# Eight forget-gate columns: from a split weight job to whole 32-bit products in four groups of output rows

## What is computed

```python
h = _rmsnorm_2(x, g_mix)                       # x: 512 x 1024, the first block's output
proj = h @ w_in                                # 1024 -> 5128 columns, split into
qa, ka, va, qb, kb, vb, fl, ga, gb = jnp.split(proj, IN_OFFSETS, axis=-1)
log_f = jax.nn.log_sigmoid(fl + b_forget)      # fl: only 8 columns, one for each head
cum = jnp.cumsum(log_f, axis=1)                # goes into the scores of the second attention
```

## Time and profile before

| | |
|---|---|
| three runs | 1702.13, 1702.26, 1707.29 us; median 1702.26 |
| span of the profiled execution | 1703.5 us |
| TensorE busy | 1661.9 us (98% of the span), 10010 matmul instructions |
| VectorE, ScalarE, GpSimd busy | 940.9, 764.6, 631.7 us |
| mean granted clock of TensorE | 0.997 |
| moved by DMA | 181.68 MB |

### The profile page before, as it was taken

The page is one execution under the profiler, slowest core; times in us unless marked ns, Lnnn a source line. Parts: engine busy times, 40 slices in busy tenths (PEclk is TensorE's granted clock), DMA queues, the critical chain, the costliest instruction groups (busy, mean ns, idle before and its releaser), DMA issues. The chain is left out here.

```text
span 1703.5 us, 26528 instructions
## 1 busy us (share of the span) xinstructions
PE 1661.9 (98%) x10010; PEld 1408.0 (83%) x10010; DVE 940.9 (55%) x1657; ACT 764.6 (45%) x1326; POOL 631.7 (37%) x439
## 2 busy tenths in 40 slices
PE   6999999999999999999999999999999999999998
PEld 4987777778888889978987788798787788989896
DVE  5326566544445258847546664777545565555552
ACT  5324554532223234566545655444445324535351
POOL 1027767342220086643113332965100227323242
PEclk9999999999999999999999999999999999999998
DMA  7322122133333223345632110224411222222221
GB/s 323 112 88 68 55 74 80 63 129 123 106 116 123 99 83 102 105 179 189 233 119 80 50 50 30 96 100 177 169 50 52 98 99 99 100 99 98 99 100 50
DMA packets 29802, 181.68 MB, mean 107 GB/s; under 512 B 3352, under 2 KB 5784, under 8 KB 10112
## 3 DMA queue, kind: packets, MB, share of 16 engines
q1 hardware_dynamic: 22136, 150.12, 24.5%
q10 hardware_dynamic: 7560, 30.09, 5.1%
HBM read 169.57 MB, written 10.50 MB: 106 GB/s over the span
## 5 line engine op out<-in xcount | busy, mean ns | idle before, releaser
L438 PE MATMUL acc<-rarena,wh 128*128 128x512 f32 (+1 forms) x1720 | 657.7, 382 | 6.9 <-DVE rarena L1792 1.3
L440 PE MATMUL acc<-rarena,wl 128*128 128x512 f32 (+1 forms) x1720 | 642.3, 373 | 0.0
L439 PE MATMUL acc<-rarena,wh 128*128 128x512 f32 (+1 forms) x1720 | 641.9, 373 | 0.0
L438 PEld LDWEIGHTS acc<-rarena,wh 128*128 128x128 f32 x1720 | 323.9, 188 | 87.7 <-issue 23.5
L440 PEld LDWEIGHTS acc<-rarena,wl 128*128 128x128 f32 x1720 | 323.8, 188 | 62.1
L439 PEld LDWEIGHTS acc<-rarena,wh 128*128 128x128 f32 x1720 | 324.2, 188 | 56.4 <-issue 0.5
L320 DVE TENSOR_TENSOR wl<-raw,wh 128x2048 fp32r<-128x2048 f32 x81 | 197.2, 2434 | 239.7 <-ACT wh L314 239.6
L314 ACT ACTIVATE wh<-raw 128x2048 fp32r<-128x2048 f32 x99 | 188.9, 1908 | 76.0 <-PE acc L440 69.4
L2555 POOL TENSOR_TENSOR wl<-raw,wh 128x512 fp32r<-128x512 f32 x78 | 105.0, 1375 | 91.2 <-ACT wh L1330 91.2
L320 POOL TENSOR_TENSOR wl<-raw,wh 128x2048 fp32r<-128x2048 f32 x18 | 82.6, 4591 | 149.4 <-ACT wh L314 149.4
L516 PE MATMUL acc<-wh,rarena 128*128 128x256 f32 x336 | 94.2, 280 | 2.7 <-DVE rarena L1792 2.5
(11 more groups left out here) (346 smaller groups left out, 3083.2 us busy)
## 6 DMA issues: line engine op xcount, KB each, us to landing
raw<-in_w SPq DMA_DIRECT2D x129, 1024.0 KB, 4.8
early<-in_wmod SPq DMA_DIRECT2D x8, 1024.0 KB, 19.8
farena<-in_gate ACTq DMA_DIRECT2D x4, 1024.0 KB, 4.8
mkv_scratch<-rarena ACTq DMA_DIRECT2D x2, 2048.0 KB, 12.0
rarena<-mkv_scratch ACTq DMA_DIRECT2D x1, 4096.0 KB, 15.0
farena<-in_rpb ACTq DMA_DIRECT2D x16, 240.0 KB, 3.8
farena<-in_x_grid SPq DMA_DIRECT2D x2, 1024.0 KB, 6.9
o_scratch<-early ACTq DMA_DIRECT2D x8, 256.0 KB, 2.0
```

The costliest lines, as they stand in the source:

```text
L438: mm(o, w[0], m[0], start=start, stop=False)
L439: mm(o, w[0], m[1], start=False, stop=False)
L440: return mm(o, w[1], m[0], start=False, stop=stop)
```

## The change

The job `FL` is taken out of the table, so that 128 jobs are left, and with it its three-part products and its split. The 8 columns come as a small array `fl` (128 x 8 x 8) by a transfer of their own, are scaled once by the norm's gains on VectorE (`fl_w`), and are multiplied as plain 32-bit numbers with the residual rows `y`, tile k into output rows 32 (k mod 4) to 32 (k mod 4) + 7 of bank `T[0]`. So four partial results, each of two tiles, stand in four groups of output rows; ScalarE copies them out (four instructions into `fl_t`), and VectorE adds them up (three additions) before it multiplies by `rstd`. The products stand ahead of the column sums; the spread moves behind the first V2 group; that group now waits for `h2_ready` tile by tile.

```diff
--- before.py
+++ after.py
@@ -23,7 +23,7 @@
 
 
 PHASES = [("V", 4, 24), ("QK", 8, 24), ("CONV", 16, 32), ("ZB", 4, 8), ("GO", 16, 32),
-          ("WO", 4, 8), ("MKV", 8, 16), ("FL", 1, 1), ("V2", 4, 16), ("DQK", 4, 8), ("FQK", 4, 8),
+          ("WO", 4, 8), ("MKV", 8, 16), ("V2", 4, 16), ("DQK", 4, 8), ("FQK", 4, 8),
           ("GO2", 12, 32), ("WO2", 4, 8), ("QM", 4, 8), ("OM", 4, 8), ("MLP", 32, 64)]
 JB, GB = {}, {}
 _j = _g = 0
@@ -189,6 +189,7 @@
         xin = view(early, 16, (KT, SEQ))
         rstd, tmp = F(24, SEQ), F(26, SEQ)
         fl_t = [F(16 + 2 * n, SEQ) for n in range(4)]
+        fl_w = F(29, KT, 8)
         ptile2, strip2, odiff = [F(0, SEQ), F(2, SEQ)], [F(4, SEQ), F(6, SEQ)], F(8, 16, 128)
         osb2 = [F(16, 128), F(16.5, 128)]
         subsq, gsub, zmask = F(17.5, 128), F(18, 128), F(19, SEQ)
@@ -882,21 +883,15 @@
                 if c == 0:
                     pe.wait_ge(s_("accy_done"), KT)
                     column_sums(S[1], acc_sq, 4, True, True).then_inc(s_("sum_done"), 1)
-                if c == 7:
-
-                    pe.wait_ge(s_("acc1_done"), KT)
-                    column_sums(S[1], acc_sq, 4, True, True).then_inc(s_("sum_done"), 1)
-
-
-            base, g = JB["FL"], GB["FL"]
-            pe.wait_ge(s_("lo_done"), base + 1)
-            acc_wait_free(pe, 0, 2, g)
+
+
+            pe.wait_ge(s_("h2_ready"), 5)
             for k in range(KT):
-                pe.wait_ge(s_("h2_ready"), k + 1)
-                last = mm3(acc[g % 2][:], wt(base % 2, k, 0), at(h2, slice(None), k), k == 0, k == KT - 1)
-            last.then_inc(s_("acc_ready"), 1)
-            pe.wait_ge(s_("ncol_ready"), 4)
-            spread(S[0], rcol, 4)
+                pe.wait_ge(s_("sq1_ready"), 2 * k + 2)
+                r = 32 * (k % 4)
+                mm(T[0][r:r + 8, :], fl_w[:, k], y[:, k], start=k < 4, stop=k >= 4)
+            pe.wait_ge(s_("acc1_done"), KT)
+            column_sums(S[1], acc_sq, 4, True, True).then_inc(s_("sum_done"), 1)
 
 
             for c in range(4):
@@ -904,7 +899,11 @@
                 pe.wait_ge(s_("lo_done"), base + 1)
                 for b in range(4):
                     token_group(base, g + b, 0, 2,
-                                lambda k, b=b: at(h2, slice(None), k, slice(128 * b, 128 * b + 128)))
+                                lambda k, b=b: at(h2, slice(None), k, slice(128 * b, 128 * b + 128)),
+                                "h2_ready" if c == b == 0 else None)
+                    if c == b == 0:
+                        pe.wait_ge(s_("ncol_ready"), 4)
+                        spread(S[0], rcol, 4)
 
 
             def project(job, u):
@@ -1391,6 +1390,7 @@
 
             act.wait_ge(s_("merged_ready"), KT)
             act.dma_start(mem, A["mem"]).then_inc(s_("mem_in"), 16)
+            act.dma_start(fl_w, A["fl"]).then_inc(s_("mem_in"), 16)
             act.wait_ge(s_("gtp_ready"), 1)
             for m in range(KT):
                 if m % 2 == 0 and m > 0:
@@ -1399,7 +1399,7 @@
                     half = slice(4 * m - 8, 4 * m - 4)
                     act.dma_start(xin[:, half], A["x_natural"][:, half]).then_inc(s_(f"xin{m - 2}"), 16)
                 if m == 1:
-                    act.wait_ge(s_("mem_in"), 16)
+                    act.wait_ge(s_("mem_in"), 32)
                     f(sqm, mem, ACT.Square).then_inc(s_("sqm_ready"), 1)
                 if m == 4:
                     act.wait_ge(s_("summ_done"), 1)
@@ -1451,13 +1451,12 @@
             act.dma_start(mkv_dram[:, 16 * 256:], mkv_all[:, 16 * 256:]).then_inc(s_("rows_spilled"), 16)
 
 
-            split_hi(act, 0, 2, JB["FL"] + 1)
             z, az, lf = fl_t[0][0:8], fl_t[1][0:8], fl_t[3][0:8]
 
 
-            act.wait_ge(s_("ncol_ready"), 4)
-            acc_wait_ready(act, 0, 2, GB["FL"])
             act.wait_ge(s_("spread_done"), 4)
+            for r in range(4):
+                f(fl_t[r][0:8], T[0][32 * r:32 * r + 8, :], ACT.Copy)
             f(rstd, S[0][:], ACT.Copy).then_inc(s_("rstd_ready"), 1)
             for c in range(4):
                 split_hi_half(act, JB["V2"] + c + 1, 0)
@@ -2106,6 +2105,8 @@
             for c in range(4):
                 split_job(v, 0, 2, JB["WO"] + c + 1)
                 if c == 2:
+                    v.wait_ge(s_("mem_in"), 32)
+                    tt(fl_w, fl_w, vec(P_MIX, 8).rearrange("p (k n) -> p k n", n=1).broadcast_to([128, KT, 8]), MUL)
                     v.wait_ge(s_("rmsm_ready"), 1)
                     link(nc.vector.reciprocal(rstd_m, rstd_m))
                     for k in range(KT):
@@ -2149,15 +2150,14 @@
                     x1_tile(KT + 1)
 
 
-            split_job(v, 0, 2, JB["FL"] + 1)
             invert(rcol, 4)
             v.wait_ge(s_("ncol_ready"), 4)
             z, m0, cum = fl_t[0][0:8], fl_t[2][0:8], fl_t[3][0:8]
-            g = GB["FL"]
-            acc_wait_ready(v, 0, 2, g)
             v.wait_ge(s_("rstd_ready"), 1)
-            free_acc(tt(z, acc[g % 2][0:8], rstd[0:8], MUL), g)
-            wait_evacuated(v, 0, 2, g)
+            tt(z, z, fl_t[1][0:8], ADD)
+            link(tt(m0, m0, cum, ADD))
+            link(tt(z, z, m0, ADD))
+            link(tt(z, z, rstd[0:8], MUL))
             link(ts(z, z, par[0:8, P_BF:P_BF + 1], None, ADD))
             ts(m0, z, 0.0, None, MIN).then_inc(s_("fl_ready"), 1)
 
@@ -2726,9 +2726,6 @@
     ga, gb = _pair_cols(win, seq(64, 4)), _pair_cols(win, seq(72, 4))
     jobs += oc + oa + [w for pair in zip(ga, gb) for w in pair]
     jobs += square(i["w_o"][0]) + square(i["w_kv_mem_2"][0], 8)
-    fl = np.zeros((KT, 128, JW), np.float32)
-    fl[:, :, 0:8] = win2[:, 3072:3080].reshape(KT, 128, 8)
-    jobs += [fl.transpose(1, 0, 2)]
     jobs += _pair_cols(win2[:, :3072], seq(8, 2)) + _pair_cols(win2[:, :3072], seq(20, 2))
     jobs += _pair_cols(win2[:, :3072], [(p, 4 + p) for p in range(4)] + [(12 + p, 16 + p) for p in range(4)])
     gates = np.ascontiguousarray(win2[:, 3080:])
@@ -2796,6 +2793,7 @@
     arrays = {
         "w": np.stack(jobs), "gate": np.stack(gate), "par": par, "ctx": feat(i["ctx"][0]), "x_grid": feat(grid), "x_natural": feat(x),
         "mem": feat(i["mem_2"][0]), "wmod": np.asarray(i["w_mod"][0])[:, :2 * D].reshape(KT, 128, 2, 4, 256).transpose(3, 2, 1, 0, 4).reshape(8, 128, KT, 256),
+        "fl": win2[:, 3072:3080].reshape(KT, 128, 8).transpose(1, 0, 2),
         "rpb": strips.reshape(16, 720), "lam": np.broadcast_to(lam, (128, 256)), "rel_bias": np.asarray(i["rel_bias_2"]),
         "gsub": np.broadcast_to(np.asarray(i["g_subln_2"][0]), (128, 128)),
         "onehot": onehot, "masked_rows": masked_rows, "cos": cos, "sin": (sin * ROOT_EIGHTH).astype(f), "wmask": wmask, "cmask": cmask, "sel": sel,
```

## The result

The changed kernel took 1708.03 us (median of 16 runs, 1705.02 to 1710.31), the kernel before 1703.56 us (16 runs, 1702.01 to 1707.49). The medians lie 4.5 us apart and the means 3.65. It is within 0.3%, but it is not the +0.8 us of the forecast, and 1708.03 lies above the range's end of 1706.2. Of the 4.9 us between 1708.03 and the forecast of 1703.1, 1.3 us is the base: the median of 1702.26 was of three runs, and 16 runs give 1703.56.

What follows compares the result with a forecast made beforehand. TensorE was taken as the bound; -5.68 (old products) + 1.86 (new) + 0.09 (group start behind the spread) + 4.52 (wait) = +0.8 us, added to the 1702.26 median: 1703.1 us, range 1700.9 to 1706.2.

Steps and rivals of the forecast that it cites:

- Part 1: Forget-logit stretch on TensorE: the 24 products leave, 5.68 us; the weight splits on ScalarE and VectorE count nothing.
- part 2: New thin products on TensorE: eight of 512 columns over four row groups take 1.86 us, 7.4 to 8.2 if not side by side.
- Part 3: New TensorE order: no wait through the second V2 group; the third could start at 828.49, 3.73 us earlier than before.
- Part 4, the wait: Third V2 group: TensorE waits 4.5 us for its bank, behind ScalarE's copies and VectorE's additions.
- spread to first copy: From the spread's start on TensorE to the first partial-result copy on ScalarE: 1.17 us.
- four copies: ScalarE copies of 8 x 512 ahead of the norms' copy: pitch 0.50 us, or 0.60 each if nothing overlaps.
- norms' copy to VectorE: From ScalarE's copy of the norms to VectorE's first operation behind it: 0.73 us.
- VectorE's chain: VectorE's additions, bias and minimum ahead of the first V2 low part: 3.69 us in all.
- low part to TensorE: First V2 bank: VectorE's low part takes 0.48 us, and TensorE starts 0.15 later.
- Part 4, its last sentence: From the third V2 group on, everything stands as before, behind TensorE; later V2 groups take 2.8 us.
- Part 5: Small column load, its scaling on VectorE and one 1 MB weight load less: all counted at 0.
- the wait that brings the clock down: Rival, behind the 4.5 us wait: one V2 group at half rate costs 2.8 us more, +3.6, 1705.9 us; chance 0.12.

## Why the prediction was wrong

Point by point, by its own steps:

- **Part 1 and part 2: right.** The 24 products and their 5.68 us are gone; the new ones took 1.84 us (forecast 1.86), and in one group of rows 6.96 (the bound there was 7.4 to 8.2, so both of its ends were too high). The estimate that the prediction worked out from the Trainium skill's figure for three column tiles (TensorE: Matmul & The Clock Gate, section "Measured speedup vs the span model") was 3.17 times and 2.6 us; the measurement decides against it, with 3.8 times for four groups. One reading in part 2 was wrong: the granted clock of 1.00 in the earlier trace rows is of 12 to 15 us, not of the half-rate row at 19.35, and it is no reading of the clock at all (last section).
- **Part 3: right.** No wait ahead of the third group; the first group took 2.89 us, the spread 0.81, the sums 0.91 instead of 0.85.
- **Part 4, the wait: right within 0.1 us.** Counted from the second group's start it was 0.10 longer than forecast. The terms: spread to first copy 1.09 (forecast 1.17); four copies 2.41 (2.00: a pitch of 0.60, the upper bound, so copies of one form did not overlap as the copy and the split behind it had); norms' copy to VectorE 0.70 (0.73); VectorE's chain 3.60 (3.69); low part to TensorE 0.52 (0.63).
- **Part 4, its last sentence: wrong.** "From the third group on everything stands as it did, behind TensorE" is the step that failed. Behind the wait TensorE's clock was 0.51, and the third group took 4.38 us in one profiled execution and 5.24 in the other, instead of 2.80. That is 1.6 to 2.4 us on top of +0.9.
- **Part 5: right as far as the trace shows.** The square that waits for the small load started at 728.74, 4.0 us earlier like everything around it, with no idle time ahead of it; no wait was added there.
- **The rivals.** The one that held was the wait that brings the clock down. That its size, +3.6 us, is also the measured one (2.2 to 4.8) is partly luck: it priced a whole group at the half rate, 2.8 us, and the group lost 1.58 us in one profile and 2.44 in the other. Its row of evidence, the half rate at the program's start, did not show a wait that brings a full clock down: nothing ran at full speed ahead of it (last section). It had a chance of 0.12, because "a V2 group is dense work". Dense work behind the wait did not prevent the fall; the clock fell in the wait or after it and stayed down while the dense work ran. The Trainium skill (TensorE: Matmul & The Clock Gate, section "HAM oscillation — how this bites in real kernels") describes this mechanism, and three of the runs agree: 4.46, 4.45 and 3.48 us idle, then half the speed. The clock also fell behind a single wait of 2.05 us, shorter than the waits that section tells of; the measurement decides.

What stays open: of the 3.6 us, 2.5 stand at this place in one execution and 3.35 in the other; how the 16 runs divide between these is not in the records, so about 1 us, or less, isn't located. Why the clock falls at different moments, in the wait or behind it, stays open too.

## What to carry to other kernels

A stall on the engine that is the bound costs more than its length if the clock falls in it or behind it: price the work behind it at both levels, and look at the granted clock in the stretch right behind a wait, not at the mean or the busy share. When products are spread over groups of output rows, the partial results have to be copied and added; put that work in a gap that exists already (here ScalarE's, ahead of the spread), and ahead of the operation that frees the next bank put only what that bank needs. The Trainium skill (TensorEngine Tiling (Array Packing), section "PSUM Bottleneck") warns that after a fourfold faster TensorE the copy out of PSUM may become the bottleneck; this case agrees in part. Four groups saved 5.1 us of products; the three more copies and three additions made the wait 3.97 us longer (4.46 against 0.49), and only with the 1.6 to 2.4 us of half speed behind it did they outweigh the saving.

## What the runs showed of the hardware

The length of a wait did not decide alone whether the clock fell. It fell with waits of 4.46, 4.45, 3.48 and 2.05 us, and with 2.00 us where another of 2.19 had ended 5.1 us earlier; it did not fall in the group behind that 2.19 us, nor with 1.36, 0.49 or 0.15. Each of these is seen in one profiled execution, and only the first two are of the same kernel. The fall came within the wait or up to 1.3 us after its end, and half speed cost 1.6 to 2.4 us each time. No limit between 1.36 and 3.48 us can be given from these runs, since 2.05 and 2.19 went different ways.

At the program's start TensorE runs at half speed for a time that differs between executions. In the profile of before, 16 instructions of line 547 take 1.94 us at 19.35 and still at 26.88; at 30.38, 32 take 1.94. In the profile after, the speed doubles earlier:

```profile
18.60 1.84 PE L548 MATMUL O<-early 128*32 128x256 f32 x16
22.05 1.07 PE L548 MATMUL O<-early 128*32 128x256 f32 x16
```

Most likely this is the lower clock again, though no trace records the clock in that time. The record of the granted clock begins, with a stretch at 1.00, where the speed doubles: at 29.05 us in the profile of before, at 20.22 after, and at 20.2 to 36.5 us in all ten traces. The 1.00 that the view by stretches gives ahead of that is no reading, because the view counts time without a record as full. The longer this half speed lasts, the later the place of the change comes. The last memory-value group ends at 815.4 to 815.8 us where the record begins at 20.2 to 20.8, at 817.8 to 819.2 where it begins at 26.2 to 29.1, and at 820.1 and 820.6 where it begins at 36.0 and 36.5. Those 5.2 us are about as much as runs of one kernel lie apart.

At the program's end the clock falls while TensorE still works: it stands at 0.50 for the last 3.3 us of TensorE's work in the profile after (from 1692.75) and for the last 1.6 us in that of before (from 1694.76).
